# Output projection: the last gate, the last probabilities, two operands of y and one finish are issued in another order, and the bias tables are copied one weight piece sooner

## What is computed

```
h    = rms_norm(x, g_pre)
proj = h @ w_in                       # q, k, v, gate of 6 + 6 heads; q, gate of 4 heads
out_a = moba_attention(...)           # 6 heads, causal softmax with a T5 relative-position bias
out_b = forgetting_attention(...)     # 6 heads, causal softmax with a cumulative forget bias
out_m = memory_attention(...)         # 4 heads into 256 memory tokens
y = concat(out * silu(gate))          # 512 x 2048
o = y @ w_out
x = x + rms_norm(o, g_post)
```

## Time and profile before

| | |
|---|---|
| median of 3 runs | 887.97 us (887.89 to 888.15) |
| profiled execution, its own time | 889.66 us |
| its span, first to last instruction | 887.9 us |
| PE busy | 865.6 us (97%) |
| DVE busy | 727.2 us (82%) |
| ACT busy | 536.8 us (60%) |
| mean granted clock of PE | 0.994 |

### The profile page before, as it was taken

How to read it: one execution, slowest core, us unless ns; L and a number is a source line. 1 busy time by engine, 2 the same in 40 slices (tenths; PEclk the granted TensorE clock), 3 DMA queues, 4 the chain that set the end, 5 groups by cost and what they waited for, 6 DMA issues and landing times.

```text
span 887.9 us, 13757 instructions
## 1 busy us (share of the span) xinstructions
PE 865.6 (97%) x5181; PEld 766.0 (86%) x5181; DVE 727.2 (82%) x1025; ACT 536.8 (60%) x918; POOL 75.9 (9%) x84
## 2 busy tenths in 40 slices
PE   9998999999999999999999999999999989999995
PEld 6997999988888888888888888888888878778884
DVE  5799789988888888888888888888888886975558
ACT  6795556565656565656565656565656575654452
POOL 0000310000000000000030303030301000000000
PEclk9999999999999999999999999999999999999999
DMA  9980586567668577657677768577644597466845
GB/s 289 303 200 23 165 181 165 148 172 159 160 171 196 137 178 176 161 163 177 153 183 170 165 171 185 144 185 170 161 121 107 172 366 259 146 214 208 289 190 189
DMA packets 179143, 161.37 MB, mean 182 GB/s; under 512 B 7353, under 2 KB 144217, under 8 KB 177670
## 3 DMA queue, kind: packets, MB, share of 16 engines
q1 hardware_dynamic: 170166, 142.66, 52.6%
q0 software_dynamic: 8704, 16.78, 13.7%
q10 hardware_dynamic: 208, 1.07, 0.4%
HBM read 152.33 MB, written 43.28 MB: 220 GB/s over the span
## 4 chain that ended last, share of the span: by engine, by line
PE 78%; DVE 12%; ACT 6%; issue 4%; DVEq 0%; POOL 0%; ACTq 0%; POOLq 0%
PE d_ps L709 19%; PE d_ps L714 10%; PE e_ps L709 10%; PE e_ps L714 5%; PE c_ps L709 5%; PE pt_ps L819 3%; DVE ring L1482 3%; PE d_ps L658 3%; PE c_ps L714 2%; PE d_ps L659 2%; PE d_ps L660 2%; ACT ring L1032 2%; PE score_ps L659 2%; PE score_ps L658 2%; PE score_ps L660 2%
## 5 line engine op out<-in xcount | busy, mean ns | idle before, releaser
L1482 DVE TENSOR_TENSOR ring<-raw,ring 128x1024 fp32r<-128x1024 f32 x134 | 164.5, 1230 | 48.6 <-ACT ring L1032 48.5
L1482 DVE TENSOR_TENSOR ring<-sums,ring 128x1024 fp32r<-128x1024 f32 x112 | 137.5, 1227 | 51.2 <-ACT ring L1032 51.1
L1032 ACT ACTIVATE ring<-raw 128x1024 fp32r<-128x1024 f32 x134 | 140.7, 1055 | 41.5 <-PE d_ps L660 15.4
L709 PE MATMUL d_ps<-late,ring 128*128 128x512 f32 x576 | 145.1, 394 | 0.0
L1032 ACT ACTIVATE ring<-sums 128x1024 fp32r<-128x1024 f32 x112 | 118.1, 1054 | 16.3 <-DVE sums L1509 13.1
L709 PEld LDWEIGHTS d_ps<-late,ring 128*128 128x128 f32 x576 | 103.4, 189 | 18.5
L714 PEld LDWEIGHTS d_ps<-late,ring 128*128 128x128 f32 x576 | 78.6, 190 | 5.7
L714 PE MATMUL d_ps<-late,ring 128*128 128x256 f32 x576 | 80.2, 282 | 0.0
L1509 DVE TENSOR_TENSOR sums<-raw 128x1024 f32<-128x1024 f32 x56 | 68.7, 1227 | 0.1
L1509 DVE TENSOR_TENSOR sums<-sums,raw 128x1024 f32<-128x1024 f32 x56 | 68.5, 1223 | 0.0
L2057 POOL DMA_DIRECT2D sum_dram<-in_w_out_dram x32 | 28.8, 900 | 421.0 <-DMA sum_dram<-in_w_out_dram 275.2
(11 more groups left out here) (387 smaller groups left out, 1915.4 us busy)
## 6 DMA issues: line engine op xcount, KB each, us to landing
raw<-in_w_in_dram SPq DMA_DIRECT2D x112, 512.0 KB, 5.7
sum_dram<-in_w_out_dram POOLq DMA_DIRECT2D x32, 512.0 KB, 7.4
raw<-sum_dram SPq DMA_DIRECT2D x32, 512.0 KB, 3.9
raw<-in_w_out_dram SPq DMA_DIRECT2D x24, 512.0 KB, 7.3
raw<-in_w_mem_kv_dram SPq DMA_DIRECT2D x16, 512.0 KB, 7.9
sum_dram<-in_w_out_dram SPq DMA_DIRECT2D x16, 512.0 KB, 6.4
sum_dram<-sum_dram SPq DMA_DIRECT2D x16, 512.0 KB, 6.1
stage<-in_x_dram SPq DMA_DIRECT2D x4, 1024.0 KB, 10.8
```

What stands on the lines that cost most here:

```text
L709: pe.matmul(bank[:], w[:, 0, k], both[:, k], start=i in (TOK_A, TOK_B) and k == 0, stop=False, skip_group_check=True)
L1032: act.activation(dst, src, ACTF.Copy).then_inc(hi_done, 1)
L1482: return dve.tensor_tensor(dst, a_, hi_.bitcast(F32), ALU.subtract)
```

## The change

Six things move. No instruction is added or removed.

1. Tables: ACT copies the bias table before `hi_mem(13)` and not after it.
2. The last gate's DVE half stands before the reciprocal and before the split of weight piece 2.
3. The last probabilities are taken ahead of the pieces split in steps 1 and 2, on both engines; piece 6 moves from step 1 to step 2.
4. C's sum (`add_y`) moves from step 8 to 7, and B's low part from 9 to 8.
5. F's high part moves from step 17 to 20, its low part from 19 to 21.
6. The last gains before step 48 and the finish of token block 2 move from step 49 to 48, with ACT's root.

```diff
-FINISH_DURING = {LAST_STEPS - SUBS + 1: (0, 2), LAST_STEPS - SUBS + 2: (1, 3)}
+GAINS_DURING = {n + (1 if n == LAST_STEPS - SUBS - 1 else 2): STEPS[n][:2] for n in range(LAST_STEPS - SUBS)
+                if n % SUBS == SUBS - 1 and STEPS[n][1] in (TOK_D, TOK_E, TOK_F, TOK_G)}
+FINISH_DURING = {LAST_STEPS - SUBS: (0, 2), LAST_STEPS - SUBS + 2: (1, 3)}
...
-    return [s for s in {0: [4], 1: [5, 6]}.get(n, [n + OUT_RING]) if s < len(STEPS)]
+    return [s for s in {0: [4], 1: [5], 2: [6, 7]}.get(n, [n + OUT_RING]) if s < len(STEPS)]
...
             hi_mem(12)
-            hi_mem(13)
             for i, (bank, lo_, hi_) in enumerate(table_banks):
                 act.wait_ge(table_made, i + 1)
                 act.activation(table[:, lo_:hi_], bank[0:NA, 0:hi_ - lo_], ACTF.Copy).then_inc(table_copied, 1)
+            hi_mem(13)
...
-                if n in (1, 2):
-                    hi_pt(last_head, n)
...
-                if n == 17:
+                if n == 20:
                     hi_y(TOK_F)
...
                     out_taken(g, i)
+                if n in (1, 2):
+                    hi_pt(last_head, n)
                 for ahead in steps_ahead(n):
                     hi_out(STEPS[ahead])
...
                 if i in (TOK_D, TOK_F, TOK_G) and packed(p):
                     merge(p, i)
+                if (p, i) == (last_pair, TOK_G):
+                    second_strip(p, i)
...
-                if n in (1, 2):
-                    lo_pt(last_head, n)
...
-                if n == 8:
+                if n == 7:
                     dve.wait_ge(y_landed[TOK_F], 32)
                     dve.wait_ge(y_raw, NH)
                     dve.wait_ge(y_sum, 1)
                     add_y(TOK_C, TOK_B, TOK_F, ALU.add)
-                if n == 9:
+                if n == 8:
                     dve.wait_ge(y_sum, 2)
                     lo_y(TOK_B, 5).then_inc(y_ready, 1)
...
-                if n == 19:
+                if n == 21:
                     lo_y(TOK_F, 9).then_inc(y_ready, 1)
...
+                if n in (1, 2):
+                    lo_pt(last_head, n)
                 for ahead in steps_ahead(n):
                     lo_out(STEPS[ahead])
                 y_work(n)
-                if n % SUBS == 1 and n > 1 and STEPS[n - 2][1] in (TOK_D, TOK_E, TOK_F, TOK_G):
-                    gain(*STEPS[n - 2][:2], 0)
-                    gain(*STEPS[n - 2][:2], 1)
+                if n in GAINS_DURING:
+                    gain(*GAINS_DURING[n], 0)
+                    gain(*GAINS_DURING[n], 1)
```

More of the change, by code:

```diff
@@ L1834, in after_operand @@
                     first_strip(p, i)
-                if p >= NM and i in (TOK_E, TOK_G):
+                if p >= NM and i in (TOK_E, TOK_G) and (p, i) != (last_pair, TOK_G):
                     second_strip(p, i)
```

## The result

| | before | after |
|---|---|---|
| median | 888.06 us (887.89 to 889.35, 4 runs) | 882.22 us (881.63 to 883.25, 4 runs) |
| ratio, with its 95% interval | | 0.9933 (0.9917 to 0.9949) |
| profiled execution, its own time | 889.66 us | 881.63 us |
| its span | 887.9 us | 879.8 us |
| PE busy | 865.6 us (97%) | 862.9 us (98%) |

The forecast was 882.0 with a range of 881.0 to 883.7. The two profiled executions stand 8.1 us of span apart and the medians 5.8.

The account below looks back on a forecast made before the run. PE, busy 97% of the span, was taken as the bound, so only its waits and DVE's late end could go. 2.27 + 1.44 + 1.1 + 1.12 = 5.9 us off a median of 887.97 gave 882.0, range 881.0 to 883.7.

Parts of the forecast that it names:

- tables: Table copies before piece 13: PE's 0.7 us wait goes but returns at product B of the first pair; worth 0.
- gate: Last gate, done in DVE's idle time before piece 2: PE's 1.20 us wait goes, gain 1.36 us.
- gate and probabilities: Last gate and last probabilities moved together: PE goes on at 729.6 instead of 731.87, gain 2.27 us.
- product B: PE's 1.28 us wait up to 757.60 goes, as B's low part directly follows piece 13; gain 1.44 us.
- product E: PE's 1.0 us wait for ACT's copy of C's result goes, as F's high part moves later; gain 1.1 us.
- margin of F: F's operand, made in steps 20 and 21, is ready 0.9 us before PE wants it, the change's smallest margin.
- finish: End of the kernel: DVE uses 1.5 us of idle time, so ACT's last square sets its sum's start; gain 1.12 us.
- The added 0.16 us for each wait: Allowance on PE's listed waits, since matmul records overlap in unbroken runs; taken between nothing and 0.24 us.
- The drain behind the table load: ACT's load for the root: the skill adds a 1.38 us drain, making the root 0.2 us late with 0.4 spare.
- return of a wait: Rival: a wait comes back elsewhere, at the probabilities or F's operand, 1 to 3 us, giving 883.0 to 885.0; chance 0.13.
- loss in the finish: Rival: the finish gains nothing, DVE's earlier finish being eaten by the root or piece 54; 883.2, chance 0.1.
- gain at the front: Rival: the front gains too, as DVE followed PE there and was not the bound; 0.8 us more, 881.2, chance 0.06.

Follow-up runs that it names:

- the two with POOL: Changed kernel with POOL instead of DVE subtracting C from G, without and with six unused matmuls ahead of the first pair's product C: 885.34 and 884.91 us.
- the first kernel with POOL: Changed kernel with the subtraction of C from G (128 x 2048) made by POOL instead of DVE, no matmuls added: 885.34 us, ratio 0.9962.

## Why the prediction was right

The time was forecast at 882.0 and came out at 882.22. That the median agrees to 0.2 us is luck, since three batches of the same changed kernel gave 882.22, 883.45 and 881.41. The sum itself held:

| term | predicted | measured | in which run |
|---|---|---|---|
| tables | 0 | 0 | 0.9999 (0.999 to 1.0008) for it alone |
| gate | 1.36 | 1.44; alone 0.00 | after; gate alone |
| gate and probabilities | 2.27 | 2.28, with 0.2 of wait left | after; probabilities alone 1.17 |
| product B | 1.44 | 1.41 | after |
| product E | 1.1 | 1.23 | after |
| margin of F | 0.9 | 0.64 | after; one step later it waits 2.00 |
| finish | 1.12 | 1.12; alone 1.14 | after; finish alone |
| rest | none | 0.12 | after |
| sum | 5.9 | 6.2 | after: 169.48 less 163.29; 163.22 to 163.32 in the five traces of the changed kernel, with or without the unused matmuls and the table edit, and 163.2 in the two with POOL |

The moves for B and E had no run of their own. For them it is shown that their waits are gone and what the trace gains there, and not what each is worth alone.

**The tables.** The sum was right and the detail wrong. I had the whole 0.7 us come back as a longer wait at 79.56, 1.1 instead of 0.3. That wait stayed at 0.29. The time came back in small pieces ahead of it: 0.22 at the split of a weight piece at 55.20, 0.24 at 75.16 for `kmv`, and the rest without a wait that the profile lists. The cover on DVE did what was said: its instruction at 59.93 had 0.48 us of idle time before, and has none now.

**The waits.** "Without the second edit the first would only have lengthened this wait" was right to the hundredth. The prediction had PE and the low part meet at 729.5, PE going on at 729.6. On the clock of the kernel before (1.84 us later) the changed trace has PE there at 729.4, the low part done at 729.5 and PE going on at 729.6. The sum of both edits is so set by where DVE ends, which is why 2.27 came out as 2.28. The added 0.16 us for each wait was on the low side: 0.24 at the gate (1.44 less 1.20), 0.13 at B, 0.22 at F, 0.28 at E (1.23 against 0.95, listed as 1.0), and 0.34 at the probabilities alone, more than the 0.24 that the prediction gave as the upper bound.

**F's operand.** From E's start at T the low part was to be done at T + 9.9 and wanted at T + 10.8. It was done at T + 10.24 and wanted at T + 10.88 (773.83, 784.07, 784.71), so the chain of ACT and DVE was mis-sized by 0.3. The margin is 0.64 in each trace of the changed kernel, and PE waits for F in none.

**The finish.** DVE's last sum follows ACT's square by 0.72 us, as forecast, and piece 54 is split at 861.6, 2 us before PE wants it. The drain behind the table load left no trace: the root starts at 856.58, when DVE's sum is done, which is 1.26 us after the load's end, and a drain of up to that size would be hidden there. The traces have another load that hides nothing, at the program's start. These are ACT's rows of the changed kernel:

```profile
1.65 1.28 ACT L1239 ACT_TABLE_LOAD   x1 [1.65 <-PEq L2094]
2.95 0.20 ACT L1239 ACTIVATE stat<-eps 128x1 f32<-128x1 f32 x1
```

The load ends at 2.93 and ACT's next instruction starts at 2.95, so no drain of 1.38 us stands behind this one. In front of the load at 863.65 in the kernel before there is none either, as ACT's copy of piece 54 ends at 863.63.

**The step from the profile to the median.** "Saved time should be the same in both" is where the prediction was loose: from one profiled execution to the other it was 8.1, from median to median 5.8. The 6.2 us saved behind 717 us are the same in every profile, but each median is drawn from executions that differ by up to 2.6 us (881.1 to 883.7 over thirteen of the changed kernel) in how PE's clock went behind the 3.6 us wait and how the first microseconds went. The medians' difference was 5.8, 4.7 and 7.8 in three batches of the changed kernel, around one value of 6.2 to 6.5. The second and the third batch ran on different chips, and a part of the spread between them may come from that. I had put what the low clock costs behind this wait down as a fixed 2.7 us. It is 1.5 to 1.9 of the span (631.91 to 632.29 less 630.43), the rest being hidden by DVE, and it is lost in full, in part or not at all.

**The rivals.** No return of a wait, but for the 0.2 us on `pT` that the prediction allowed, and no loss in the finish. A gain at the front did not come from the tables. What looks like one in the first profile differs between executions of one kernel.

The lowest median of these runs is that of the changed kernel with fourteen unused matmuls ahead of product C: 881.23 us, and within 0.4 us of it in all five runs. The changed kernel without them came to 881.41 in its best batch, so what the matmuls bring is mainly that the time no longer depends on the clock's course.

## What to carry to other kernels

Work out moved instructions as chains: where the waiting engine would arrive, where the releasing engine would end, and take the later. Consecutive waits on one engine can be one debt; here removing the first alone gave 0.00, and both together paid only because the second's own releaser had become early enough. Before a change of under 1% is judged by medians, look for a place where the clock sometimes falls, and compare traces from an event behind it, or hold the clock up in both kernels.

## What the runs showed of the hardware

- At one and the same idle time of PE, 3.58 or 3.59 us, the granted clock was at 1.2 GHz until about 92 us, until before 90 us, or not at all, in executions of the same kernel (spans 881.6, 879.8 and 879.3). The long one costs 1.6 us against none, the short one 0.6. What decides between them was not found. The length of the idle time alone doesn't: in the first kernel with POOL the clock stayed up at an idle time of 3.45 us and fell at a later one of 2.60 us.
- In the first microseconds, the pace of PE's warm-up matmuls doubled at 4.6 us in one execution and after 6 us in another, with a granted clock listed as 1.00 for both; 0.7 us of span go with it. Two traces of the changed kernel differ in it as well: the matmul with `gain_rows` stands at 5.94 in one and at 6.61 in the other.
- POOL's difference of 128 x 2048 fp32 elements took 4.59 us, and a two-input DVE instruction that started 0.02 us behind it took 6.72 instead of 2.28.
- ACT started its next instruction 0.02 us after the end of a table load of 1.28 us (2.93 and 2.95 us, changed kernel).
- In an unbroken run of matmuls that follow at 0.23 us, an idle time in the trace costs 0.13 to 0.34 us more than it shows, and one of about 0.2 us can be missing from PE's list altogether (the changed kernel at 727.75 us).
